# New turn order in the mixer phases of a hybrid decoder step, and 26 added products of ones per layer

## The reference

```
for layer in 0, 1:
  h = RMSNorm(x); c = h @ w_in          # 1024 -> columns of three groups
  RWKV-7 group (6 heads of 64): token shift, low-rank decay, recurrence with a matrix state
  retention group (4 heads): rotary q and k, chunked decayed attention, state
  Mamba-2 group (6 heads, state 128): causal conv of 4, chunked scan, state
  x += concat(groups) @ w_out
  x += SwiGLU (layer 0) or top-2-of-8 SwiGLU experts (layer 1) of RMSNorm(x)
y = RMSNorm(x)
```

## Time and profile before

| what | value |
|---|---|
| median of 3 runs | 1403.95 us (1399.22 to 1405.0) |
| the profiled execution's own time | 1401.54 us |
| its span, first to last instruction | 1399.7 us |
| mean granted TensorE clock | 0.934 of 2.4 GHz |
| TensorE, VectorE, ScalarE, GpSimd busy | 95%, 67%, 51%, 10% of the span |
| layer 0: last input slot ends, out-projection starts | 211.0 us, 311.5 us |
| layer 1: the same | 777.3 us, 875.6 us |

### The profile page before, as it was taken

The page is one execution under the profiler, slowest core; times in us unless marked ns, Lnnn a source line. Parts: engine busy times, 40 slices in busy tenths (PEclk is TensorE's granted clock), DMA queues, the critical chain, the costliest instruction groups (busy, mean ns, idle before and its releaser), DMA issues.

```text
span 1399.7 us, 26188 instructions
## 1 busy us (share of the span) xinstructions
PE 1326.7 (95%) x10133; PEld 1156.3 (83%) x10133; DVE 938.2 (67%) x1492; ACT 720.0 (51%) x1097; POOL 136.0 (10%) x160
## 2 busy tenths in 40 slices
PE   5999999989999999899999998989999999999996
PEld 4899887768999999889988876877787787778775
DVE  5485755445655556748676453559888897898887
ACT  5633454114433343363335421467778777777774
POOL 1031310030000000002121002000100100100011
PEclk9999998559999999899999865999999999999997
DMA  6321320035444444133122002639879897897982
GB/s 251 117 93 33 107 99 16 12 108 213 149 151 164 151 151 151 39 109 108 48 92 98 32 12 76 231 120 337 311 263 330 309 338 254 317 335 260 351 302 81
DMA packets 62919, 235.05 MB, mean 168 GB/s; under 512 B 7264, under 2 KB 7488, under 8 KB 62048
## 3 DMA queue, kind: packets, MB, share of 16 engines
q1 hardware_dynamic: 59760, 217.61, 44.5%
q0 software_dynamic: 2336, 12.81, 2.4%
q10 hardware_dynamic: 720, 3.18, 0.6%
HBM read 225.48 MB, written 8.09 MB: 167 GB/s over the span
## 4 chain that ended last, share of the span: by engine, by line
issue 33%; PE 19%; ACT 2%; DVE 2%; POOL 1%; POOLq 0%; DVEq 0%; ACTq 0%
PE bank L562 4%; PE bank L568 3%; PE bank L570 2%; PE bank L569 2%; PE bank L1049 1%; POOL x L2686 1%; PE bank L722 1%; PE bank L733 1%; PE bank L729 1%; ACT whi L1323 0%; PE bank L937 0%; PE bank L589 0%; PE bank L798 0%; PE bank L984 0%; PE bank L950 0%
## 5 line engine op out<-in xcount | busy, mean ns | idle before, releaser
L1323 ACT ACTIVATE whi<-wraw 128x1024 fp32r<-128x1024 f32 x410 | 433.0, 1060 | 395.9 <-PE bank L570 309.8
L1795 DVE TENSOR_TENSOR wlo<-wraw,whi 128x1024 fp32r<-128x1024 f32 x410 | 500.8, 1227 | 201.1 <-ACT whi L1323 196.5
L568 PE MATMUL bank<-hh,whi 128*128 128x320 f32 x608 | 202.2, 333 | 16.6 <-DVE wlo L1795 4.7
L569 PE MATMUL bank<-hl,whi 128*128 128x320 f32 x608 | 191.8, 315 | 0.0
L570 PE MATMUL bank<-hh,wlo 128*128 128x320 f32 x608 | 191.7, 315 | 0.0
L1242 PE MATMUL bank<-whi,hh 128*128 128x512 f32 (+1 forms) x384 | 147.3, 384 | 3.7 <-DVE wlo L1795 3.2
L1244 PE MATMUL bank<-wlo,hh 128*128 128x512 f32 (+1 forms) x384 | 143.4, 373 | 0.0
L1243 PE MATMUL bank<-whi,hl 128*128 128x512 f32 (+1 forms) x384 | 143.0, 373 | 0.0
L568 PEld LDWEIGHTS bank<-hh,whi 128*128 128x128 f32 x608 | 117.6, 193 | 29.6 <-issue 11.0
L569 PEld LDWEIGHTS bank<-hl,whi 128*128 128x128 f32 x608 | 118.5, 195 | 0.0
L570 PEld LDWEIGHTS bank<-hh,wlo 128*128 128x128 f32 x608 | 117.8, 194 | 0.0
(11 more groups left out here) (411 smaller groups left out, 2285.0 us busy)
## 6 DMA issues: line engine op xcount, KB each, us to landing
wraw<-in_w SPq DMA_DIRECT2D x410, 512.0 KB, 5.0
smb<-in_s_ssm POOLq DMA_DIRECT2D x2, 1536.0 KB, 7.7
out_o_ssm<-smb POOLq DMA_DIRECT2D x2, 1536.0 KB, 12.0
cst<-in_consts ACTq DMA_DIRECT2D x1, 2161.0 KB, 12.9
srw<-in_s_rwkv POOLq DMA_DIRECT2D x2, 768.0 KB, 4.8
out_o_rwkv<-srw POOLq DMA_DIRECT2D x2, 768.0 KB, 3.6
x<-in_x SPq DMA_DIRECT2D x1, 1280.0 KB, 5.7
out_y<-x SPq DMA_DIRECT2D x4, 320.0 KB, 2.2
```

The source lines that it names most:

```text
L568: mm(out, hi, rh, start=first, stop=False)
L569: mm(out, hi, rl, start=False, stop=False)
L1323: af(whi[:, ring % HI, :], wraw[:, POS[ring], :], ACT.Copy).then_inc(S("slot_hi"), 1)
L1795: tt(wlo[:, POS[ring], :], wraw[:, POS[ring], :], whi[:, ring % HI, :].bitcast(F32), ALU.subtract).then_inc(S("slot_split"), 1)
```

## The change

The four merge lists are replaced by new ones. ACT's, DVE's and POOL's hold the same turns in another order; PE's has 26 more, named `fill`. Each is one product of ones by ones, 128 x 128 by 96 columns, f32, into columns 320 to 416 of bank 6, which nothing reads. The first waits until all tiles of the projection have been read from their banks. Three stand before the output turn of Mamba block 2, two behind it on either side of the last turns of `rw1` and `mb2`, two before retention 2's state product (L950), seven behind that product, two before the first late turn, and ten among the late turns.

Behind the last `in` turn PE had `rw0` 9, `rt0` 4, `mb1` 4, `cb1` 4, `tok1` 3, `mb2` 5, `rw1` 11, `rt1` 7, `rt2` 7 and `late` 8 turns; now `rw0` 7, `rt0` 5, `mb0` 3, `mb1` 5, the rest as before, and 26 `fill`. The output turn of Mamba block 2 was the 34th turn behind the last `in`, with 28 behind it; now it is the 54th, with 37 behind it, 23 of them `fill`.

```diff
--- before.py
+++ after.py
@@ -147,37 +147,40 @@
 SQ_ACT = 6
 SUM_BANKS, RS_BANK = (0, 1, 2), 3
 PE_TURNS = """
-    in in in in in in in in prep in in in in in in prep in in in in in in prep in in in in in in inv2 inv1 in
-    inv0 in inv1 inv2 inv0 in inv2 in prep inv2 inv0 inv1 in in inv1 inv0 inv2 prep inv1 in inv0 inv2 in inv1
-    inv0 cb2 cb2 sS sS sS inv0 in inv0 in inv0 inv1 cb2 cb2 sS inv0 dt tok2 inv1 inv0 tok2 inv1 in inv0 dt in in
-    in tok2 in in inv1 rw2 in in rw2 inv1 in in inv1 nS in cb0 nS rw2 in nS rw2 in rw2 in mb0 cb0 cb0 in tok0 in
-    cb0 rt0 tok0 mb0 in in rt0 rw2 mb0 rt0 in in mb0 in mb0 tok0 in rw0 mb1 rw0 in in rw0 rw0 mb1 rw0 mb1 rt0
-    rw0 mb1 rw0 rw0 cb1 rw0 mb1 cb1 cb1 rw0 cb1 tok1 mb2 tok1 tok1 rw0 rt0 rt0 rw1 mb2 rt0 rw1 mb2 rt1 rw1 rw1
-    rt1 mb2 rt1 rw1 rt1 rt1 rw1 rt1 mb2 rt1 rw1 rw1 rt2 rw1 rt2 rw1 rt2 rw1 rt2 rt2 rt2 late late rt2 late late
-    late late late late
+    in in in in in in in in in in prep in in in in prep in in prep in in in in inv0 in in inv1 inv2 in inv0 in
+    in inv2 inv0 inv1 inv0 inv2 inv1 inv0 inv1 inv0 inv1 inv2 inv1 inv2 in inv2 inv1 prep inv0 inv1 prep inv1
+    inv0 cb2 cb2 sS sS cb2 sS cb2 inv0 tok2 inv0 tok2 inv0 inv1 inv0 inv1 sS inv1 in in in dt in tok2 in rw2 in
+    in dt in in in in in in rw2 in rw2 in in in in rw2 in rw2 nS cb0 rw2 in nS in in nS in in mb0 cb0 cb0 rt0
+    cb0 in in mb0 rt0 tok0 tok0 in tok0 in rw0 in in rw0 in rw0 in rw0 in in rw0 rt0 mb0 rw0 rt0 rw0 rw0 rt0 rt0
+    cb1 rw0 mb0 rw0 rt0 cb1 mb0 rw0 rt1 mb1 cb1 cb1 rt1 tok1 tok1 tok1 fill rt1 rw1 mb1 rw1 mb1 rt1 mb1 rt1 rt1
+    rw1 rw1 rt1 rw1 mb1 rw1 fill rt2 mb2 rw1 rw1 mb2 fill rt2 rw1 mb2 rt2 rw1 mb2 fill rw1 mb2 fill rt2 fill
+    fill rt2 fill fill fill fill fill fill fill rt2 fill fill late fill late fill fill fill late fill fill late
+    fill late late fill rt2 late fill fill late
 """
+FILL_COLS = 96
+N_FILL = PE_TURNS.split().count("fill")
 ACT_TURNS = """
-    dt in in in in prep prep in in in in prep prep prep in in in in prep in in prep prep in in in in in in in in
-    in in in in in in in in prep conv in in prep conv prep in in conv in in sS dt dt tok2 conv tok2 dt in in in
-    in conv tok2 in conv in conv in rw2 in in in in in rw2 rw2 in in mb0 mb0 tok0 in in tok0 mb0 in in rt0 in
-    mb0 mb0 tok0 in mb1 rw0 mb1 in mb0 rw2 mb1 rt0 rt0 rw0 mb1 rw0 rw0 mb1 rw0 mb1 tok1 mb2 tok1 tok1 mb2 rt0
-    rw0 mb2 rw1 rt0 mb2 rt1 rt1 rt1 rw1 rt1 mb2 mb2 rt1 rw1 rw1 rw1 rt2 rw1 rt2 rt2 rt2 rt2
+    in dt in prep in in prep in in in in in in prep prep prep prep in in in in prep prep in in in in in in in in
+    in in in in prep prep tok2 tok2 sS in in dt dt in in tok2 prep conv in in dt conv in in in in conv in in
+    conv rw2 conv in in conv in in in rw2 conv in rw2 in in in in in in mb0 mb0 in in tok0 mb0 tok0 tok0 in in
+    in rw0 in in rw2 rt0 rw0 rt0 rt0 rw0 rt0 rw0 mb0 rw0 rt0 mb0 mb0 mb1 tok1 rw0 tok1 tok1 mb1 rt1 mb1 rw1 rt1
+    rt1 mb1 rt1 rt1 mb1 rw1 mb1 mb2 mb2 rw1 mb2 rw1 rt2 rw1 mb2 mb2 mb2 rw1 rt2 rt2 rt2 rt2
 """
 DVE_TURNS = """
-    prep in in in in in in in prep in in in in in in prep in in in in prep in prep prep in prep prep in in inv2
-    inv2 inv1 inv1 in inv0 inv0 inv1 in inv1 inv0 inv2 inv0 inv2 in inv2 in prep inv0 inv1 inv2 in inv2 inv0
-    inv1 conv conv conv conv inv1 in conv conv inv0 inv2 conv conv inv1 inv0 inv2 in conv inv0 conv conv conv
-    cb2 cb2 inv1 inv0 inv0 inv0 in inv1 cb2 cb2 conv conv dt conv conv inv0 dt inv1 dt dt dt dt dt dt inv0 inv1
-    dt dt dt inv0 dt dt in conv conv conv conv in conv conv conv conv in conv conv inv1 conv conv rw2 in xs inv1
-    inv1 in xs nS nS xs nS cb0 nS rw2 in nS nS rw2 in cb0 cb0 mb0 cb0 in rt0 rt0 mb0 rt0 rt0 in in in in rw2 mb0
-    rw2 mb0 rw2 mb0 mb0 mb0 mb0 mb0 mb0 rw0 mb1 rw0 rw0 mb0 rw2 mb1 rw0 mb1 mb1 mb1 mb1 mb1 mb1 rw0 rw0 cb1 cb1
-    cb1 mb1 mb1 rw0 cb1 mb1 mb2 rw0 rt0 rw0 rw0 rt0 rw0 rw1 mb2 rt0 rt0 mb2 mb2 rt0 rt1 rw1 rt1 rw1 rt1 rt1 mb2
-    mb2 mb2 rw1 rt1 rt1 mb2 mb2 rt1 rt1 rw1 mb2 rt1 rt2 rt2 rt2 rt2 rw1 rw1 rw1 rw1 rw1 rt2 rt2 rt2 late late
-    rt2 rt2 late rt2 late late late late late
+    prep in in in in in in in in in in prep in in in prep in prep prep prep prep prep in in inv0 inv0 in inv0 in
+    inv0 prep inv1 inv1 inv2 inv2 inv1 inv2 inv1 inv2 in inv0 in in inv2 inv0 inv1 inv0 inv2 inv1 inv0 inv1 inv0
+    inv1 inv2 inv1 inv2 inv2 in in inv1 inv0 inv1 inv1 inv0 cb2 cb2 cb2 cb2 inv0 inv0 inv0 inv1 inv0 inv1 inv1
+    in in dt dt dt dt in conv conv conv conv dt dt dt dt rw2 dt dt dt in conv conv dt conv conv dt in conv conv
+    conv conv conv in conv conv conv in conv conv conv conv xs in rw2 conv conv conv conv in conv conv conv conv
+    in rw2 nS xs rw2 cb0 rw2 nS rw2 in nS xs nS in nS nS in cb0 cb0 rt0 cb0 mb0 rt0 rt0 in mb0 rt0 in in in in
+    rw0 rw0 rw0 rw2 rw0 mb0 mb0 rw0 rw0 rt0 cb1 rt0 mb0 mb0 mb0 mb0 rt0 rw0 rt0 cb1 rt0 mb0 mb0 rw0 rt1 mb0 rt1
+    rw0 cb1 rw0 cb1 rt1 rt1 mb1 rw0 rw1 mb1 mb1 mb1 mb1 mb1 rt1 mb1 mb1 rw1 rt1 rw1 rt1 rt1 rt1 rw1 mb1 mb1 rt2
+    mb1 rt2 rt2 rw1 mb2 mb2 rt2 mb2 mb2 rw1 mb2 mb2 mb2 rw1 mb2 mb2 rw1 rw1 mb2 rw1 rt2 rt2 rt2 late late late
+    late late late rt2 rt2 late rt2 late
 """
 POOL_TURNS = """
-    prep prep shift conv conv prep conv conv conv conv xv conv conv xv xv xv xv mb0 rt0 mb1 mb2 rt1 rt1 conv mb1
-    rt2 rt2 mb2 rt2 mb2
+    prep prep shift prep conv xv conv conv conv conv conv conv conv xv xv xv xv mb0 rt0 rt1 mb1 rt1 conv mb1 rt2
+    mb2 rt2 mb2 rt2 mb2
 """
 
 
@@ -620,6 +623,19 @@
                     m = mm(B[q][0:n, 0:1], htmp[:, 0, c0:c0 + n], C("ones", 0, 1), start=True, stop=True)
                 m.then_inc(S("sq_ready"), 1)
 
+            def idle_product():
+
+                mm(B[6][:, T:T + FILL_COLS], ones_n[:, :], ones_n[:, 0:FILL_COLS], start=True, stop=True)
+
+            def fill(l):
+
+                for j in range(N_FILL):
+                    yield
+                    if j == 0:
+                        pe.wait_ge(S("a_read"), NA * (l + 1))
+                        pe.wait_ge(S("in_read"), NI * (l + 1))
+                    idle_product()
+
             def dense(l):
 
                 for j in range(WIN):
@@ -1051,7 +1067,7 @@
                     m.then_inc(S("mb_ds"), 1)
 
             def parts_of(l):
-                p = {"in": dense(l), "prep": prep(l), "dt": steps(l), "sS": sample_states(l), "nS": new_states(l),
+                p = {"fill": fill(l), "in": dense(l), "prep": prep(l), "dt": steps(l), "sS": sample_states(l), "nS": new_states(l),
                      "late": late_states(l)}
                 for b in range(3):
                     p |= {f"inv{b}": inverse(l, b), f"cb{b}": reads(l, b), f"tok{b}": tokens(l, b), f"rw{b}": rwkv(l, b),
```

## The result

The kernel after took 1439.61 us (median of 4 runs, 1435.26 to 1440.55), the kernel before 1401.59 on the same chip (4 runs, 1397.14 to 1405.0): ratio 1.0267, 95% interval 1.0227 to 1.0307. It is slower by 38 us, 40 us above the forecast and 19 above the upper end of the range. Medians take all runs of a kernel; ratios and their intervals leave out runs more than 1.5% above its fastest. (Three slips above, which no step uses: the input projection has 30 slots, 60 turns, not 31; in GpSimd's list the first `xv` turn passes five `conv` turns, not six; the earlier trace rows shows a fifth wait over 0.2 us, of 0.23.)

A forecast was written before the change was run, and what follows sets the result against it. TensorE was taken to set the pace, at half clock in much of each mixer phase's second half. Terms -23.9 + 18.1 + 1.5 = -4.3 us against 1401.5 gave 1397.2, as a median 1399.6 us; range 1369 to 1421.

The forecast's parts named there:

- The order behind the last slot: Turns after each layer's last projection slot: running them ahead of the 8-column run at full clock gives -23.9 us, bounds 0 and -31.9.
- Up to the last slot: Reordered turns before each layer's last projection slot: same total TensorE work, so no gain or loss, bounds -11 to +11 us.
- Work that crosses the last slot: Turns now left behind the last projection slot, some 3 us at full clock: moved and not added, cost nothing.
- The 26 products: The fills of each layer, behind the last projection slot: 9.0 us per layer, +18.1 us in all; bounds 4.8 to 12.2 per layer.
- ten among the late products: Ten fills among late products that ran back to back: 0.47 us each at half clock, +4.7 us per layer.
- The wait of the Mamba norm: TensorE's wait for VectorE before the next block's first product: +1.5 us for both layers, between -2 and +5.
- The rule weighed: Idle gaps between matmul bursts drop the clock, so filling them keeps it up: time of the rival where the clock holds.
- The third: Clock falls early behind the last slot and stays: none of the 31.9 us comes; 1425 median, put at 1421; chance 0.22.
- its finer one: Sign in the new profile: Mamba 0's output products already at half clock would mean the third case holds.
- clock 1.0 for three quarters ahead of the run: Sign: from last projection slot to 8-column run, full clock for three quarters or more; only what follows at 0.5.
- 4.8 us: Sign: time from retention 2's state product (L950) to the first late product, 2.2 us before, should be near 4.8.
- 16 us: Sign: the late products, with ten fills among them, should spread from 11.5 to 16 us.

## Why the prediction was wrong

**The order behind the last slot, -23.9 us: the step that failed.** It rested on reading and the earlier trace rows together as "the 8-column run takes the clock". Moving the run late left 25 and 44 us at half ahead of it; leaving seven eighths of it out moved the fall by under 2 us. So turns set ahead of it win nothing by that. In place of a gain of 23.9 the order alone has more time at half, over the four stages 11.5 us in one profiled execution and 27.3 in the other, a loss of 5 to 12 us. With the 26 products the tails have 161.5 us at half against 141.2. The warning stood in the same step (the clock fell ahead of the run at 233.2 and at 793) and was priced at a quarter, where it was the whole.

**Up to the last slot, priced at nothing (bounds +-11): held.** The content of the two input parts is 379.2 us before, 379.1 with the new order and 379.1 in the kernel after. It is a balance: 4.9 us of busy time left these parts and 4.8 of idle time came (5.7 to 7.7 and 4.0 to 6.8). Layer 1's input part also has 8 us more at half in the kernel after.

**Work that crosses the last slot, priced at nothing ("moves and is not added"): the second step that failed.** The tails gained 13.5 us of content by the order alone (69.7 to 76.6 and 69.1 to 75.7), 9.0 busy and 4.4 idle, and the parts that the work had left gave nothing back. The sum had no term for this.

**The 26 products, +18.1 us: right in sum, in part by luck.** 17 to 21 us measured. The equal price of 8 and 96 columns held. From L966 to the first late product it is 309.05 - 300.59 = 8.5 us, of which 304.20 to 309.05 = 4.8 as forecast. Undersized was the step "ten among the late products, 10 x 0.47": the late products spread from 11.5 to 18.7 us (309.05 to the end of the last at 327.8), 7.2 more and not 4.7, as the ten stand in six groups, each of which costs 0.48 beside the 0.43 of each fill. Oversized was the price of the first 14 of a layer, which cost 0.14 each at full clock, half of the prediction's 0.28. The two errors cancel.

**The wait of the Mamba norm, +1.5:** the wait went from 1.1 to 1.7 us in layer 0's tail and from 0.8 to 1.5 in layer 1's, near the 0.75 a layer that was forecast.

**The rule weighed,** that gaps between bursts cost the clock (the Trainium skill, TensorE: Matmul & The Clock Gate, Part 1, "HAM oscillation"): filling more than half of the idle time in the tail left the clock where it was, 0.64 to 0.65. As the prediction took the rule it would have risen. What was filled are short gaps, for no wait in the tail before was longer than 1.9 us; a long gap was not tested. The 13.60 us at half with TensorE busy for all 13.60, in the kernel after, speak the same way as the earlier trace rows did.

**The rivals.** The third came true in its condition (41 of the 73 us ahead of the run at half, and 27 of 67 in layer 1) and in its finer one (Mamba 0's output products, at 222.6 us, ran in a first dip to half clock), but not in its price: 1425 was the sum of the fills and the waits, and most of the missing 14 us are the content of the order, 13.4, which no case contained. The range failed for that reason: all its cases took the work that crosses the last slot as free. Of the signs named, "clock 1.0 for three quarters ahead of the run" failed, "4.8 us" came, "16 us" came as 18.7, and no TensorE wait in the input parts reached several microseconds: the longest was 1.8, and the new idle time there is many small ones.

**What stays open.** Which property of the chunk products makes the clock fall: filling short gaps, dense fills and leaving out most of the run of 8 columns did not stop the falls. Waits alone do not explain them either: the fall at 233.2 us comes behind a wait of 1.1 us, that at 816.9 behind 10.2 us without any, and the one after the 48 products behind 13.3 (7.00 and 6.30, all busy). The share of the tail at half lay between 0.46 and 0.78 from kernel to kernel with no rule found. About 4 of the 13.4 us of the order's content are busy time whose cause was not found.

## What to carry to other kernels

Split every stretch into content and time at half clock before pricing a change of order: content came out the same within 1 us from tail to tail and from one execution of the new order to the other, the clock's share did not. Do not take an instruction that stands where the clock falls for the cause; move it or leave it out alone, which takes one run. Do not price work that moves to another stretch at nothing: here its new place grew by 13.5 us and its old place gave nothing back, as idle time took its room.

## What the runs showed of the hardware

- A product of ones costs 0.46 us in a row of seven and 0.91 alone between products of another shape, both at half clock. Of the 0.91 some 0.48 are the price of the break, paid once for a group of one to three.
- The same order of turns ran from 1394.7 to 1429.8 us in four runs (the new order without fills) and from 1405.7 to 1430.3 in twelve more, the kernel before from 1394.6 to 1409.7 in 28 beside those twelve. Two profiled executions of that order agreed in content within 1 us and differed by 16 us in their time at half clock: one profiled execution tells the content of an order well and its time badly.
- A run of 48 dense products at full clock (0.14 us each) was followed by 6.3 us of full clock, and then by 59 us of half.
- The clock also came back in a tail without any projection product near: at 284.4 us in the kernel before, and at 255.0 us in the kernel after, behind 13.6 us at half.
